# The prompt's recurrences: five doubling steps on 64-position blocks, row vectors spread by DMA, the mask added on GpSimd

## The reference, cut to what matters

```python
z = h @ w_in[l]
mixer = concat(retention(4 heads) | mLSTM(4 heads) | gated DeltaNet(4 heads) | NSA(4 query heads)) @ w_out[l]
x = x + RMSNorm_post(mixer)
# retention, mLSTM, DeltaNet all have this shape, over chunks of the sequence:
o = scores(q, k) * decay @ v + (q * decay) @ S
S = S * decay + (k * decay)^T @ v
# DeltaNet: v is replaced by the solution d of (I + N) d = beta * (v - decay * k S),
# N strictly lower triangular, N[i, j] = beta[i] * decay[i, j] * (k[i] . k[j])
y = RMSNorm(o) per head, times gain and gate
```

## Time and profile before

| what | value |
|---|---|
| median of three runs | 4205.48 us |
| profiled execution | 4212.83 us |
| its span | 4211.0 us |
| PE busy in the span | 3765.2 us (89%) |
| DVE busy | 1950.8 us (46%) |
| ACT busy | 1286.9 us (31%) |
| POOL busy | 418.9 us (10%) |
| the stage, layer 0 | 451.4 to 760.4 us |

### The profile page before, as it was taken

How to read it: one execution, slowest core, us unless ns; L and a number is a source line. 1 busy time by engine, 2 the same in 40 slices (tenths; PEclk the granted TensorE clock), 3 DMA queues, 4 the chain that set the end, 5 groups by cost and what they waited for, 6 DMA issues and landing times. The chain is left out here.

```text
span 4211.0 us, 55742 instructions
## 1 busy us (share of the span) xinstructions
PE 3765.2 (89%) x22236; PEld 3203.9 (76%) x22236; DVE 1950.8 (46%) x3830; ACT 1286.9 (31%) x2902; POOL 418.9 (10%) x296
## 2 busy tenths in 40 slices
PE   5999698688979999999979987977898899999997
PEld 4888587445658999997768876864475789999875
DVE  3234477663444333335541436776533443333455
ACT  2111255452222221123331114554432322211343
POOL 0035101002201000000000540010021100000000
PEclk9999799798989999999989998997899999999999
DMA  7344322305432222255543433122152422222654
GB/s 246 118 142 161 99 64 61 104 6 204 170 104 89 76 70 66 76 180 206 212 160 105 166 114 97 60 70 79 40 232 105 157 66 76 67 69 84 221 195 179
DMA packets 302046, 504.85 MB, mean 120 GB/s; under 512 B 67381, under 2 KB 226774, under 8 KB 297201
## 3 DMA queue, kind: packets, MB, share of 16 engines
q1 hardware_dynamic: 296523, 426.06, 31.3%
q0 software_dynamic: 4608, 67.11, 3.9%
q10 hardware_dynamic: 656, 8.13, 0.6%
HBM read 386.90 MB, written 129.63 MB: 123 GB/s over the span
## 5 line engine op out<-in xcount | busy, mean ns | idle before, releaser
L1033 PE MATMUL ps<-h_hi,fu_hi 128*128 128x344 f32 x2112 | 682.3, 323 | 10.1 <-DVE h_lo L1255 7.3
L1035 PE MATMUL ps<-h_hi,fu_lo 128*128 128x344 f32 x2112 | 677.6, 321 | 0.0
L1034 PE MATMUL ps<-h_lo,fu_hi 128*128 128x344 f32 x2112 | 677.1, 321 | 0.0
L564 PE MATMUL ps<-zi_whi,h_hi 128*128 128x468 f32 (+1 forms) x1152 | 432.9, 376 | 50.7 <-DVE zi_wlo L645 50.7
L1033 PEld LDWEIGHTS ps<-h_hi,fu_hi 128*128 128x128 f32 x2112 | 398.0, 188 | 14.1 <-DVE h_lo L1255 7.8
L1035 PEld LDWEIGHTS ps<-h_hi,fu_lo 128*128 128x128 f32 x2112 | 398.8, 189 | 0.0
L1034 PEld LDWEIGHTS ps<-h_lo,fu_hi 128*128 128x128 f32 x2112 | 398.2, 189 | 0.0
L568 PE MATMUL ps<-zi_wlo,h_hi 128*128 128x468 f32 (+1 forms) x1024 | 384.2, 375 | 0.0
L569 PE MATMUL ps<-zi_whi,h_lo 128*128 128x468 f32 (+1 forms) x1024 | 384.0, 375 | 0.0
L1059 PE MATMUL ps<-fd_whi,fd_fhi 128*128 128x512 f32 x704 | 278.4, 395 | 15.0 <-DVE fd_flo L1272 14.2
L564 PEld LDWEIGHTS ps<-zi_whi,h_hi 128*128 128x128 f32 x1152 | 217.5, 189 | 80.3 <-DVE h_lo L641 51.9
(11 more groups left out here) (633 smaller groups left out, 6964.2 us busy)
## 6 DMA issues: line engine op xcount, KB each, us to landing
w_ahead<-w_ffn_down SPq DMA_DIRECT2D x44, 1024.0 KB, 5.8
z<-zi_z SPq DMA_DIRECT2D x112, 234.0 KB
zi_h<-z SPq DMA_DIRECT2D x64, 384.0 KB, 4.6
f_all<-fu_f SPq DMA_DIRECT2D x44, 516.0 KB, 3.4
w_ahead<-w_ffn_gate SPq DMA_DIRECT2D x44, 512.0 KB, 4.8
w_ahead<-w_ffn_up SPq DMA_DIRECT2D x44, 512.0 KB, 6.1
fd_raw<-w_ffn_down SPq DMA_DIRECT2D x22, 1024.0 KB, 5.6
zi_raw<-w_in SPq DMA_DIRECT2D x24, 936.0 KB, 5.6
```

What stands on the lines that cost most here:

```text
L564: nc.tensor.matmul(out, rows_hi, w_hi[:, i % 2, k, c0], start=(k == 0), stop=False)
L1033: nc.tensor.matmul(out, up_hi[f % 2][:, j, k, :], h_hi[:, k, seg], start=(k == 0), stop=False)
L1034: nc.tensor.matmul(out, up_hi[f % 2][:, j, k, :], h_lo[:, k, seg], start=False, stop=False)
L1035: m = nc.tensor.matmul(out, up_lo[f % 2][:, j, k, :], h_hi[:, k, seg], start=False, stop=(k == KD - 1))
```

## The change

The inverse is built for the two 64-position blocks of each tile alone (five steps, `STEPS`), and the second half of the solution follows from the first by substitution: `x1_up` (lower half), `n_x1` (its effect on the upper half), a subtraction on VectorE (`rest`) and `x2_up`, with two evictions on ScalarE. These three groups are 64x64 products; the one `delta` group goes. Beta enters through the exponent of the gate's mask (`LB`), so the product of keys with beta, its turn on TensorE and its eviction go, and the values are loaded as they are by a DMA. The row sums on TensorE go: the row vectors are stored to `r_rows` once per layer, and two DMAs per tile spread them to all partitions; GpSimd adds the mask (`shifted`), two additions of 128x512 per tile. The order of the programs is written anew.

```diff
 LEV = 7
+STEPS = LEV - 2
...
+    def rows_in(t):
+        if t >= 2:
+            sp.wait_ge(S("shifted"), t - 1)
+        for k in range(2):
+            sp.dma_start(R.brow[:, t % 2, k]..., env["r_rows"][k, t].partition_broadcast(P)).then_inc(S(f"rows_in{t % 2}"), 16)
...
+    for k, ready in enumerate(("decay_rows", "max_rows")):
+        sp.wait_ge(S(ready), 1)
+        sp.dma_start(env["r_rows"][k]..., R.rows[:, k]).then_inc(S("rows_stored"), 16)
+    sp.wait_ge(S("rows_stored"), 32)
+    rows_in(0)
+    rows_in(1)
     beside(Loads(sp, env["kept"]))
     for t in range(NT + 1):
         if t + 2 < NT:
             heads_in(t + 2)
+            rows_in(t + 2)
...
+    def shifted(n):                                    # GpSimd
+        pool.wait_ge(S(f"rows_in{n % 2}"), 32 * (n // 2 + 1))
+        if n:
+            pool.wait_ge(S("p_g"), n)
+            pool.wait_ge(S("p_m"), n)
+        G_.tensor_tensor(R.w2[:], R.brow[:, n % 2, 0], mask, ALU.add)
+        G_.tensor_tensor(R.wm[:], R.brow[:, n % 2, 1], mask, ALU.add).then_inc(S("shifted"), 1)
+    shifted(0)
+    shifted(1)
     for p in range(NT):
+        if p + 2 < NT:
+            shifted(p + 2)
...                                                     # TensorE
-            pe.wait_ge(S("xt_up"), 6 * p + 6)
-            pe.wait_ge(S("mi"), p + 1)
-                m = T.matmul(ps[:, 6, h * HD:h * HD + HD], R.XT[:, qo, h, :], R.rvp[:, h, :], ...)
-            m.then_inc(S("delta"), 1)
+                m = T.matmul(ps[lower, 6, ...], R.XT[lower, qo, h, lower], R.rvp[lower, h, :], ...)
+            m.then_inc(S("x1_up"), 1)
...
+                m = T.matmul(ps[upper, 6, ...], R.NLT[lower, qo, h, upper], R.dl[lower, h, :], ...)
+            m.then_inc(S("n_x1"), 1)
...
+                m = T.matmul(ps[upper, 6, ...], R.XT[upper, qo, h, upper], R.rvp[upper, h, :], ...)
+            m.then_inc(S("x2_up"), 1)
...
-            turn("k", n, [pair(R.kb, k) for k in range(2)])
-            T.matmul(ps[:, 4, :], R.pick[:, n, :], R.mrow[:]..., start=True, stop=True)
-            T.matmul(ps[:, 5, :], R.pick[:, n, :], R.grow[:]..., start=True, stop=True).then_inc(S("row_sums"), 1)
...                                                     # ScalarE, end of the loop
         if t == NT:
             sample_softplus()
...
+            head_sums(2, p, "squared12")
+            act.wait_ge(S("m_o"), p + 1)
+            head_sums(1, p, "m_squared")
...
-            act.wait_ge(S("m_o"), t + 1)
-            head_sums(1, t, "m_squared")
...                                                     # VectorE
-            link(V.tensor_tensor(R.w2[:], ps[:, 5, :]..., every(R.maskT[:]), ALU.add))
-            link(V.tensor_tensor(R.wm[:], ps[:, 4, :]..., every(R.maskT[:]), ALU.add), S("shifted"))
...
+            updated(5)
+            ...                                         # r_S, two additions
         if post:
             dve.wait_ge(S("r_squared"), p + 1)
             dve.wait_ge(S("m_squared"), p + 1)
             dve.wait_ge(S("squared12"), p + 1)
             link(V.tensor_scalar(R.ss12[:, qo], R.ss12[:, qo], EPS, None, ALU.add), S("sq_in"))
```

More of the change, by code:

```diff
@@ L1637, in prompt_tensor @@
             for k in range(2):
-                m = T.matmul(ps[:, 7, k * P:k * P + P], R.KBT[:, qo, k, :], R.Sgdn[:, k, :], start=True, stop=True)
+                m = T.matmul(ps[:, 7, k * P:k * P + P], R.TG[:, qo, 2 + k, :], R.Sgdn[:, k, :], start=True, stop=True)
             m.then_inc(S("k_state"), 1)
+        if main:
+            updates(1)
+        if post:
             pe.wait_ge(S("om"), p + 1)
@@ L1672, in prompt_tensor @@
         if main:
-            products(3)
+            products(4)
         if prep:
[L1675 to L1680, removed]
-            turn("k", n, [pair(R.kb, k) for k in range(2)])
-            pe.wait_ge(S("rows"), 1)
+            pe.wait_ge(S("turn_read"), turn_number("g", n))
             if n:
                 pe.wait_ge(S("p_m"), n)
-            T.matmul(ps[:, 4, :], R.pick[:, n, :], R.mrow[:].rearrange("p h n -> p (h n)"), start=True, stop=True)
-            T.matmul(ps[:, 5, :], R.pick[:, n, :], R.grow[:].rearrange("p h n -> p (h n)"), start=True, stop=True).then_inc(S("row_sums"), 1)
+            for k in range(2):
+                for h in range(H):
+                    m = T.matmul(score(k, h), own(R.TG[:, qo, 2:4], h), own(R.TG[:, qo, 2 - 2 * k:4 - 2 * k], h), start=True, stop=True)
+            m.then_inc(S("g_scores"), 1)
         if main:
-            products(4)
+            updates(4)
             if post:
                 pe.wait_ge(S("gi"), p + 1)
-            pe.wait_ge(S(f"values_in{q}"), 80 * (t // 2 + 1))
+            pe.wait_ge(S(f"values_in{q}"), 96 * (t // 2 + 1))
+            pe.wait_ge(S("p_m"), t + 1)
             if t:
@@ L1699, in prompt_tensor @@
             m.then_inc(S("r_o"), 1)
[L1700 to L1716 removed]
+            products(5)
+            if post:
+                pe.wait_ge(S("g_o"), p + 1)
+            for k in range(2):
+                m = T.matmul(ps[:, 6, k * 130:k * 130 + 130], R.TM[:, q, k, :], R.Caug[:, k, :], start=True, stop=True)
+            m.then_inc(S("m_inter"), 1)
             if post:
@@ L1722, in prompt_tensor @@
             updates(5)
-            if post:
-                pe.wait_ge(S("g_o"), p + 1)
-            if t:
-                pe.wait_ge(S("m_state"), t)
-            for k in range(2):
-                m = T.matmul(ps[:, 6, k * 130:k * 130 + 130], R.TM[:, q, k, :], R.Caug[:, k, :], start=True, stop=True)
-            m.then_inc(S("m_inter"), 1)
+        if prep:
+            pe.wait_ge(S("p_g"), n + 1)
+            pe.wait_ge(S("turn_read"), turn_number("r", n))
+            for k, src in ((0, R.TM), (1, R.TR)):
+                for h in range(H):
+                    m = T.matmul(score(k, h), own(src[:, qo, 2:4], h), own(src[:, qo, 0:2], h), start=True, stop=True)
+            m.then_inc(S("scores"), 1)
+            pe.wait_ge(S("xt0"), n + 1)
+            turn("x", n, [R.XT[:, qo, h, :] for h in range(H)])
+        if main:
             pe.wait_ge(S("r_read"), t + 1)
@@ L1738, in prompt_tensor @@
             m.then_inc(S("m_dstate"), 1)
-        if prep:
-            pe.wait_ge(S("xt0"), n + 1)
-            turn("x", n, [R.XT[:, qo, h, :] for h in range(H)])
-        if main:
-            updates(6)
 def prompt_scalar(kit, env, R, act, data):
@@ L1911, in prompt_vector @@
     link(V.memset(R.mp[:, 0], 0.0))
-    link(V.tensor_reduce(R.own[:], ident[0:32, 0:32].rearrange("p (t h) -> p h t", h=H), AX.X, ALU.add))
-    link(V.tensor_reduce(R.tile[:], ident[0:32, 0:32].rearrange("p (t h) -> p t h", h=H), AX.X, ALU.add))
-    link(V.tensor_copy(R.pick[:], bc(R.tile[:], NT, [32, NT, P])))
     dve.wait_ge(S("gates_in"), 16 * 7)
```

315 lines of the change are left out of this document (151 added, 164 removed).

## The result

The changed kernel takes 4225.27 us in the median (4219.55 to 4233.42), the kernel before 4207.9 on the same chips (4198.74 to 4220.31): a ratio of 1.0043, 95% interval 1.0031 to 1.0055, or 13 to 23 us more. The forecast was 4211, five more, in a range of 4168 to 4238. The sign and the mechanism came as forecast, the size was too small by about 13 us. By the prediction's own bound of 21 us both five and eighteen are no change, so the sign alone proves little; what bears the forecast out is the inside of the slots.

What follows compares the result with a forecast made beforehand. TensorE nearly full, but the inverse's chain of steps sets the slot. Per layer −1.0 − 7.7 − 5.2 − 1.0 + 2.5 + 14.8 = +2.4; two layers about +5 on 4205.5: 4211, range 4168 to 4238.

Steps and rivals of the forecast that it cites:

- The restart: From a tile's last subtraction to the end of the next first mask: 9.25 us in place of 4.15, +5.1.
- The sixth step and the row sums: Per steady slot: inverse's sixth step goes, −5.07; step 4 loses row sums and mask work, down to 4.3, −2.67.
- The 64x64 groups: Three groups of 64x64 products replace one of 128x64: +0.4 per slot; shape changes, up to 1.3, only in the range.
- The moved work: TensorE work moved into steps 3 and 5 (step 4's gate work, the retention state): +0.9 per slot, between 0 and 2.8.
- The clock: After TensorE's idle at a slot's head, 3.4 us at half clock: +1.15 per slot, between 0 and 3.4.
- A steady slot: Sum of terms for one slot, 2 to 6: −0.2 us each, five together −1.0 per layer.
- Rival C: VectorE and GpSimd meet: additions take 1.86, r_y starts 0.7 later, more low clock; +26, 4237 us; chance 0.24.
- Slot 1: Second slot of each layer: −5.2 us, between −6.4 and −4.4; nothing taken for loads queued behind the store's wait.
- Slot 7 and the last tile: Slot 7 +2.5 us; epilogue behind the last tile +14.8, between +9 and +18, including 2.5 for two table loads.
- The prologue and slot 0: Per layer: prologue −1.0 us (10.1 against 11.1), between −2.7 and +3.3; slot 0 −7.7; together −8.7.
- Rival A: The wait for r_y does not come, power and scalings overlap other work: −64, 4147 us; chance 0.08.
- B: Wait comes, but clock stays 1.00, 64x64 groups hide, moved work 0.5, DMAs land early: −31, 4180 us; chance 0.18.

Runs made afterwards that it cites:

- late_y: Changed kernel with r_y of tile t-2 moved on VectorE behind the right side of slot t, the last tile's left in place; 4178.77 us, ratio 0.9931.
- before_late: Kernel before, six steps and row sums kept, with squares closed behind the last subtraction and r_y ahead of r_C; 4334.92 us, ratio 1.0298.
- fill: Changed kernel with 44 unread transposes filling TensorE's idle at the head of each slot from the third on; 4216.64 us, ratio 1.001.
- dve_mask: Changed kernel with the mask added on VectorE behind the second subtraction instead of on GpSimd, DMAs kept; 4219.41 us, ratio 1.0014.
- sample_loads: Changed kernel with the 80 or so small sample loads issued on SyncE behind tile 2's loads instead of ahead; 4227.12 us, ratio 1.0036.
- early_sq: Changed kernel with the squares closed behind the fourth subtraction in all slots but the last, r_y unmoved; 4207.08 us, ratio 0.999.

## Why the prediction was right, and where its sum was off

- The restart (9.25 forecast, 9.23 measured) and its cause: right, shown from both sides by late_y and before_late.
- The sixth step and the row sums: the step is gone; step 4 is 4.85, not 4.3, so it gave 2.12, not 2.67.
- The 64x64 groups: +1.05 against +0.4; the change of shape, kept for the range, belonged into the sum. The moved work, taken at +0.9, came to little: at full clock (fill) steps 1, 2, 3 and 5 changed by +0.33, +0.90, +0.20 and −0.22, together 1.21, against 0.4 + 0.9 = 1.3 for both terms. So two misses cancel, and that is luck; no run parts the two.
- The clock: 0.84 against 1.15 per slot in its cost. In the slots the granted 0.50 lasted 3.4 or 6.8 us, so the upper bound of the stretch came often, but it cost less: TensorE was still idle for the first 2.3 us of such a stretch (576.15 to 578.45), and in most slots the second step lost nothing.
- A steady slot: 0.07 us shorter than before, against the forecast 0.2, near in part by luck, since step 4 gave 0.55 less and the clock cost 0.31 less. Slots 2 to 6 together are at +0.4 against −1.0, because single slots were longer (31.39 and 31.81 us in the first profile); why they were is open.
- GpSimd's additions in the steady slots: 1.25 against 1.24, no meeting: right. Rival C in its place falls; its mechanism decided slot 1 where that was longest.
- Slot 1: the step that failed. "I take nothing for them", the loads queued behind the wait for the store, cost 3.2 us per layer in the mean, through late rows, the meeting on the port and a fall of the clock; in layer 0 of the first profile 1.01 us is TensorE's wait for r_zq, which is loaded by the same queue. Slot 1 is short in both runs that take the meeting away (25.7 in dve_mask, 26.0 in sample_loads), so the cause of the long slot is shown. Whether the total lost the same through it is open: the time fell in dve_mask and not in sample_loads.
- Slot 7 and the last tile: +3.5 and +15.6 against +2.5 and +14.8, within 1 us each. In the last tile one term had the wrong reason: the 2.5 for the table loads was 3.44, and 2.81 of it a wait of ScalarE for VectorE's d_col.
- The prologue and slot 0: −10.2 against −8.7; 0.7 of the difference comes from one long slot 0 of the kernel before. From the row vectors to the end of the second addition go 9.1 us (475.38 to 484.44) against the forecast 10.1.
- Rival A falls: the wait came. Of B the cheaper moved work and a part of the clock came, but the 64x64 groups were dearer and slot 1 cost what B had nothing for.

## What to carry to other kernels

When a step is taken out of a chain, write down the new chain through every engine up to the first instruction of the next round: an operation that nobody waits for, r_y here, costs its whole wait if it stands in an in-order engine ahead of one that is waited for. Place such an operation behind the work of the chain, and then look at what stands behind the next engine's part of it, as the eviction behind the scalings did in late_y. Of a queue that gets a new wait, price what stands behind the wait at the place where it lands, not only at its deadline.

## What the runs showed that I had not expected

Two engines that share a port can be kept apart by a stall: early_sq shortened the wait and had r_y run into GpSimd's addition (1.86 us against 0.96). In each meeting shown here the VectorE operation ended behind GpSimd's addition, by its own usual time less about 0.14 us (r_y 0.82 of 0.96, the rotary product 0.55 of 0.69, r_den 0.03 of 0.17): it had waited for the addition and not run slower beside it, whatever its size. An idle of 1.8 us of TensorE was followed by half clock in some slots (layer 1 of the changed kernel at 2593.42), not in others: late_y, with 1.8 us of idle at each head, has slots of 27.51 us at a mean granted clock of 1.00, of 28.43 at 0.94 and of 29.65 at 0.88. And the rest of the program, which the change does not touch, differed by 5.6 us between the two profiles of the kernel before, as much as the effects argued over in slot 1.
